# Softplus tiles in two rounded parts for the running sums, and attention scores in one VectorE pass

## The reference

```python
# sparse head: q, k, slope
logits = einsum(q, k) * 64 ** -0.5 - slope * |t - s|      # minus infinity where not selected
p = softmax(logits)
# stick-breaking head: keys s before query t only
z = einsum(q, k) * 64 ** -0.5
log_keep = log_sigmoid(-z)                                # = -softplus(z)
after = reverse cumulative sum of log_keep - log_keep
w = exp(log_sigmoid(z) + after)
```

## Time and profile before

| | us |
|---|---|
| median of 3 runs | 1257.1 (1255.69 to 1260.04) |
| the profiled execution's own time | 1256.63 |
| its span | 1254.8 |
| TensorE busy | 1225.6 |
| VectorE busy | 746.6 |
| ScalarE busy | 505.9 |
| GpSimd busy | 81.1 |
| mean granted TensorE clock | 0.995 |

### The profile page before, as it was taken

One profiled execution on the slowest core, in us unless ns is written; L12 is line 12 of the kernel. 1 busy time (PEld: TensorE's weight loads), 2 busy tenths in 40 slices (PEclk: granted clock), 3 DMA queues, 4 the chain that ended last, 5 costly groups with the idle time before them and its releaser, 6 DMA issues.

```text
span 1254.8 us, 15910 instructions
## 1 busy us (share of the span) xinstructions
PE 1225.6 (98%) x6200; PEld 993.1 (79%) x6200; DVE 746.6 (60%) x1029; ACT 505.9 (40%) x700; POOL 81.1 (6%) x122
## 2 busy tenths in 40 slices
PE   5999999999999999999999999999999999999998
PEld 4789888888888888878788875568788888888887
DVE  7998887674554444575588948755843333333332
ACT  5443426514314314334432258852551441432431
POOL 0010000000000000140000002114000000000032
PEclk9999999999999999999999999999999999999999
DMA  9558791844453454412232210003233323332211
GB/s 321 191 134 237 277 335 60 293 132 166 177 168 126 174 176 154 159 57 86 82 101 92 81 64 1 1 1 101 68 111 94 97 101 101 100 99 76 94 67 67
DMA packets 132696, 157.54 MB, mean 126 GB/s; under 512 B 19784, under 2 KB 113152, under 8 KB 132608
## 3 DMA queue, kind: packets, MB, share of 16 engines
q1 hardware_dynamic: 125328, 153.82, 36.8%
q10 hardware_dynamic: 7312, 2.96, 1.0%
HBM read 151.39 MB, written 4.19 MB: 124 GB/s over the span
## 4 chain that ended last, share of the span: by engine, by line
PE 87%; DVE 6%; DMA 3%; ACT 2%; issue 1%; ACTq 0%; POOL 0%; SPq 0%; DVEq 0%
PE psum L1800 85%; PE psum L1804 2%; DMA ada_first<-in_ada_w 1%; DVE ada_ring L1170 1%; DVE ada_acc_b L1191 1%; DMA w_raw<-in_mlp_w 1%; DMA raw_bn<-in_ssm_b_im 1%; DVE h_lo L1409 1%; ACT pT L1111 1%; DVE w_lo L1376 1%; DVE ada_acc L1191 0%; DMA y_t<-y_scratch 0%; DVE cat_f L1528 0%; DVE sumsq L1170 0%; DVE work L1390 0%
## 5 line engine op out<-in xcount | busy, mean ns | idle before, releaser
L1800 PE MATMUL psum<-h_hi,w_hi 128*128 128x512 f32 (+1 forms) x872 | 344.1, 395 | 0.6 <-DVE w_lo L1376 0.6
L1800 PE MATMUL psum<-h_lo,w_hi 128*128 128x512 f32 (+1 forms) x872 | 340.9, 391 | 0.0
L1800 PE MATMUL psum<-h_hi,w_lo 128*128 128x512 f32 (+1 forms) x872 | 340.6, 391 | 0.0
L786 ACT ACTIVATE w_hi<-w_raw 128x2048 fp32r<-128x2048 f32 x92 | 174.4, 1896 | 285.4 <-PE psum L1800 284.8
L1376 DVE TENSOR_TENSOR w_lo<-w_raw,w_hi 128x2048 fp32r<-128x2048 f32 x92 | 212.2, 2307 | 89.1 <-ACT w_hi L786 88.3
L1800 PE MATMUL psum<-a_hi,w_hi 128*128 128x512 f32 x512 | 202.5, 396 | 0.0
L1800 PE MATMUL psum<-a_hi,w_lo 128*128 128x512 f32 x512 | 202.1, 395 | 0.0
L1800 PE MATMUL psum<-a_lo,w_hi 128*128 128x512 f32 x512 | 202.1, 395 | 0.0
L1800 PEld LDWEIGHTS psum<-h_hi,w_hi 128*128 128x128 f32 (+1 forms) x872 | 164.1, 188 | 38.6 <-issue 3.6
L1800 PEld LDWEIGHTS psum<-h_hi,w_lo 128*128 128x128 f32 (+1 forms) x872 | 164.1, 188 | 35.0
L1800 PEld LDWEIGHTS psum<-h_lo,w_hi 128*128 128x128 f32 (+1 forms) x872 | 164.2, 188 | 33.3
(11 more groups left out here) (318 smaller groups left out, 1345.2 us busy)
## 6 DMA issues: line engine op xcount, KB each, us to landing
w_raw<-in_mlp_w SPq DMA_DIRECT2D x64, 1024.0 KB, 5.4
ada_l_ring<-in_ada_w SPq DMA_DIRECT2D x64, 384.0 KB, 5.9
w_raw<-in_cd_w_in SPq DMA_DIRECT2D x14, 1024.0 KB, 5.2
ada_ring<-in_ada_w SPq DMA_DIRECT2D x17, 384.0 KB, 6.0
ada_more<-in_ada_w SPq DMA_DIRECT2D x15, 384.0 KB, 4.6
ada_first<-in_ada_w SPq DMA_DIRECT2D x5, 1024.0 KB, 15.3
w_raw<-in_ab_w_in SPq DMA_DIRECT2D x4, 1024.0 KB, 7.3
w_raw<-in_ab_w_out SPq DMA_DIRECT2D x4, 1024.0 KB, 8.4
```

What stands on the lines that cost most here:

```text
L786: act.activation(w_hi[n % 2][:, :, 0:w], raw[n % 2][:, :, 0:w], ACT.Copy).then_inc(hi_ready, 1)
L1800: return nc.tensor.matmul(o, lhsT, rhs, start=start, stop=stop, **kw)
```

## The change

The softplus tile of a head is split by VectorE, behind the causal cut, in a high part in the rounded format (`sp_high`, one buffer) and a low part, the rest (`sp_low`, in the place of the tile). The running sums are then two rounded products, high and low, where one fp32 product was, with `tri` and `ones` copied once into the rounded format. TensorE waits for the split (`sp_parts`) instead of `sp_ready`.

The scores take one VectorE pass per query block: it adds the distance to the score in PSUM, multiplies with the slope, writes the result and keeps its minimum. For that the query copies carry the factor -(1/8) / slope of their head (`q_scale`, written once by eight memsets). What is written is the negated logit, so the exponential takes a scale of -1 with the minimum as its bias.

```diff
+    sp_low = [place(f"sp_low{i}", [P, W1], F32R, offset=idx_at + 4 * W1 * (2 + i)) for i in range(2)]
+    sp_high = place("sp_high", [P, W1], F32R, offset=ada_ring_at + 4 * 10 * P)
+    tri_r = place("tri_r", [P, P], F32R, offset=ada_ring_at + 4 * 20 * P)
+    ones_r = place("ones_r", [P, P], F32R, offset=ada_ring_at + 4 * 21 * P)
...
+    q_scale = small[:, 44:48]
...
@@ scalar: prob_exps, and the copies of the projection @@
-                act.activation(probs(step, i), probs(step, i), ACT.Exp, bias=small[:, i:i + 1],
+                act.activation(probs(step, i), probs(step, i), ACT.Exp, bias=small[:, i:i + 1], scale=-1.0,
                                accum_out=small[:, 8 + i:9 + i]).then_inc(p_exp, 1)
...
+                    ct = 2 * half + r
+                    if name == "qc":
+                        act.wait_ge(q_scale_ready, 1)
+                        copy_tile(t0 + r, qc[:, ct, :], scale=q_scale[:, ct:ct + 1])
+                    else:
+                        copy_tile(t0 + r, dst[:, ct, :], scale=HD ** -0.5 if name == "qd" else 1.0)
...
@@ vector, behind ada_gate(a, 16) @@
+        for t in range(4):
+            for g2 in range(2):
+                own(dve.memset(q_scale[HD * g2:HD * g2 + HD, t:t + 1], -(HD ** -0.5) / SLOPES[2 * t + g2]))
+        settle()
+        dve.sem_inc(q_scale_ready, 1)
...
@@ selected_distances @@
+            own(dve.tensor_copy(tri_r[:, :], tri[:, :]))
+            own(dve.tensor_copy(ones_r[:, :], ones[:, :]))
+            settle()
             dve.sem_inc(dsel_ready, 1)
...
+        def softplus_parts(head):
+            dve.wait_ge(sp_ready, NB * (head + 1))
+            own(dve.tensor_copy(sp_high[:, :], sp_sb[head % 2][:, :]))
+            settle()
+            dve.tensor_tensor(sp_low[head % 2][:, :], sp_sb[head % 2][:, :], sp_high[:, :].bitcast(F32), SB)\
+               .then_inc(sp_parts, 1)
...
@@ score_rows @@
-                dve.scalar_tensor_tensor(out=probs(step, i), in0=dsel[:, sel_at[i]:sel_at[i] + w],
-                                         scalar=-SLOPES[step], in1=bank[4 + n % 2][:, 0:w],
-                                         op0=M, op1=A).then_inc(s_used, 1)
-                dve.wait_ge(s_used, NB * step + n + 1)
-                dve.reduce_max(small[:, i:i + 1], probs(step, i), AX_X, negate=True)\
-                   .then_inc(max_ready, 1)
+                dve.tensor_tensor_reduce(out=probs(step, i), in0=dsel[:, sel_at[i]:sel_at[i] + w],
+                                         in1=bank[4 + n % 2][:, 0:w], scale=SLOPES[step], scalar=3.0e38,
+                                         op0=A, op1=ALU.min, accum_out=small[:, i:i + 1]).then_inc(max_ready, 1)
...
@@ vector, loop over the steps @@
             if step < H:
                 score_rows(step)
+            softplus_parts(step - 1)
             if step >= 3 and step % 2 == 1:
                 out_lo((step - 3) // 2)
...
@@ tensor: scores @@
-                pe.wait_ge(s_used, NB * step + n - 1)
+                pe.wait_ge(max_ready, NB * step + n - 1)
...
@@ stick_sums @@
-            s_ = sp_sb[pr % 2]
-            pe.wait_ge(sp_ready, NB * (pr + 1))
+            if pr == 0:
+                pe.wait_ge(dsel_ready, 1)
+            pe.wait_ge(sp_parts, pr + 1)
+            parts = (sp_high, sp_low[pr % 2])
...
-                last = mm(o[:, 0:w], tri[:, :], s_[:, z_at[j]:z_at[j] + w], True, j == NB - 1)
+                for part, s_ in enumerate(parts):
+                    last = mm(o[:, 0:w], tri_r[:, :], s_[:, z_at[j]:z_at[j] + w], part == 0, part == 1 and j == NB - 1)
                 for j2 in range(j + 1, NB):
                     w2 = (NB - j2) * P
-                    last = mm(o[:, w - w2:w], ones[:, :], s_[:, z_at[j2]:z_at[j2] + w2], False,
-                              j2 == NB - 1)
+                    for part, s_ in enumerate(parts):
+                        last = mm(o[:, w - w2:w], ones_r[:, :], s_[:, z_at[j2]:z_at[j2] + w2], False,
+                                  part == 1 and j2 == NB - 1)
```

More of the change, by code:

```diff
@@ L258, in trunk @@
     assert at[0] <= nc.sbuf_usable_end, (at[0], nc.sbuf_usable_end)
+    sp_low = [place(f"sp_low{i}", [P, W1], F32R, offset=idx_at + 4 * W1 * (2 + i)) for i in range(2)]
+    sp_high = place("sp_high", [P, W1], F32R, offset=ada_ring_at + 4 * 10 * P)
+    tri_r = place("tri_r", [P, P], F32R, offset=ada_ring_at + 4 * 20 * P)
+    ones_r = place("ones_r", [P, P], F32R, offset=ada_ring_at + 4 * 21 * P)
+    assert W1 == 10 * P and ada_ring_at + 4 * 22 * P <= ada_ring_at + 4 * (ADA_RING + 1) * ADA_Q
     p_at = [0, P, 3 * P, 6 * P]
@@ L455, in trunk @@
     sp_ready = sem("sp_ready")
+    sp_parts = sem("sp_parts")
     r_ps = sem("r_ps")
@@ L461, in trunk @@
     s_ps = sem("s_ps")
-    s_used = sem("s_used")
+    q_scale_ready = sem("q_scale_ready")
     max_ready = sem("max_ready")
@@ L875, in _ @@
         act.sem_inc(c_ready, 1)
+        qc = qk["qc"]
         def copy_tile(t, dst, src=None, **kw):
@@ L1094, in _ @@
                         continue
-                    copy_tile(t0 + r, dst[:, 2 * half + r, :], scale=HD ** -0.5 if name in ("qd", "qc") else 1.0)
+                    ct = 2 * half + r
[4 more added lines that the diff above has]
+                        copy_tile(t0 + r, dst[:, ct, :], scale=HD ** -0.5 if name == "qd" else 1.0)
                     if n == index_first and r == 0:
```

## The result

The changed kernel takes 1273.2 us (median of 4 runs, 1272.8 to 1274.7) against 1256.5 for the kernel before on the same chip (1255.7 to 1260.0); the ratio of all their runs is 1.0110, with an interval of 1.0077 to 1.0144. It is slower, by some 14 to 17 us. The forecast was 1259 with a range up to 1267: the likelier side (slower, given 0.54) came true, the size did not. The profiled execution has a span of 1271.0 us (before 1254.8) and a mean granted clock of 0.982 (before 0.995). Some single executions, of the kernel before too, take 1267 to 1275 us at a mean clock near 0.983, so times are compared as medians.

The account below looks back on a forecast made before the run. TensorE's order bounds the step, with a serial softplus chain half a microsecond behind. First step +3.4, clock +0.85, middle steps -5 x 0.02, last step -0.5, end -1.2: +2.5 on 1256.6 gives 1259 us, range 1255 to 1267.

Parts of the forecast that it names:

- the shortening: Per step, start of the sums to end of the last subtraction: 1.36 us shorter, though TensorE's sums save 1.9.
- The first step's late start: First head's sums wait for the split behind the tail of the score rows: start at 751.4, 3.4 us late.
- The end: After the last step only TensorE counts: its last sums take 3.4 us and not 4.58, -1.2.
- (a): Split's rounding copy on VectorE runs at one element a cycle: 0.66 us more in all eight steps, +5.3, 1264; chance 0.16.
- (e): Split's subtraction too runs at 0.82, so the split leaves the chain: step 11.36, 1254; chance 0.10.
- rival (c): Fused score pass on VectorE saves nothing: 1.38 x 7 = +9.7 us, 1269; chance 0.08.
- rival (b): Narrow rounded products in TensorE's sums cost the fp32 rate, 0.22: 8 x 0.45 = +3.6 us, 1263; chance 0.20.
- S = X+3.8: In each step the last subtraction ends (S) about 3.8 us after the sums start (X); before it was 5.16.
- rival (d): New TensorE idle time ahead of the sums lowers the clock in every step: 6 x 0.85 = +5 us, 1264; chance 0.08.
- From S to the next sums: Per step, end of the last subtraction through softplus, maximum, score passes, absolute value and split to the next sums: 8.22 us.
- The first, +0.85 forecast for the clock: First step's sums and what follows run partly at half speed: double the old slow spell, +0.85 us.
- The last, -0.5 forecast: Last step has no score rows: a period of 11.8 us against 12.27, -0.5.

Follow-up runs that it names:

- the filled kernel: Changed kernel plus eight unused 128-column fp32 products in TensorE's wait ahead of each step's sums; 1262.1 us, ratio 1.0042 (measured again: 1262.1, 1.0034).
- the pair: Changed kernel and the same with eight unused products in TensorE's wait, measured again side by side: 1274.7 us (9 runs) against 1262.1 (12 runs).

## Why the prediction was wrong

**Right, by the rows.** That the gain of 1.9 us in TensorE's sums would turn into a wait for the split: the wait is there in every step. That the shortening arrives as 1.36 us and not 1.9: with the clock up it was 1.38 (13.72 against 12.34). The first step's late start, 3.4 forecast, was 3.3 to 3.65. The end, -1.2, was -1.4. The copy at 0.82 and the subtraction at 1.48 were 0.83 and 1.49, so rivals (a) and (e) are out. The two tail passes took 0.63 (805.58 to 806.21), forecast 0.72; rival (c) is out. Here the Trainium skill (Vector Engine (DVE) Microarchitecture Reference, "Points that are easy to get wrong") warned that the two-source form S2S2D2_STT halves its throughput when both sources lie in SBUF and are not bf16. The fused pass has one source in PSUM and is as fast as the plain one (0.42 for 256 columns), and the maximum-and-add, with two fp32 sources in SBUF, takes the 1.49 us of the plain subtraction. The narrow rounded products: at full clock a pair of 128 columns takes 0.17 us (792.73 to 792.90), 0.06 to 0.11 each, so rival (b) is out too.

**The step that failed: S = X+3.8.** I let the sums run at full clock after 1.4 us of idle. In the filled kernel, where the clock is up, it holds: the first block takes 1.33, and S is X+3.70 (793.10 + 2.17 - 791.57). In the changed kernel the first subtraction starts at X+2.64 (798.76) and not X+1.60, and the last one ends at S = 801.24, X+5.12. This is +1.3 a step over the forecast and +1.4 over the filled kernel, and the mean steps differ by as much (13.76 - 12.34): 7.1 of the 8.65 us in the middle five intervals, and 12.6 us in the medians of the pair. It was rival (d). I gave it 0.08, on one observation, that 2 us of idle precede the drop of the earlier trace rows, which I read as if 1.4 us could then not suffice; one run shows that 1.38 can (and 1.46 need not), and the wait came out at 2.06 anyway. And I priced it at 0.85 a step, what the old first step had lost. There the slow spell began ahead of the sums and was over by 750, within their first 2 us. In the changed kernel it covers the first 3 us of the sums, and their end starts the next chain.

**A smaller term of the same sum.** From S to the next sums I had 8.22, and it was 8.54 (801.24 to 809.78), in the filled kernel 8.64 (795.27 to 803.91). The cut, which I put at 1.02 and off the path ("done since about S+5.5"), takes 1.62 beside the absolute value, ends at S+6.1 and holds the copy back; the absolute value itself was 0.98 in this step, against 0.82. The steps of 12.34 against the forecast's 12.02 show 0.32, and that is 1.9 us over the six intervals in which an absolute value runs beside the cut (in the last one the cut takes 1.03 and the term is nothing: 842.95 to 850.92, 7.97 for the 7.99 of the forecast). It also fed the first error, since it lengthens the wait, which was 2.06 and not 1.4.

**The first and the last interval.** The first, +0.85 forecast for the clock, was +1.23. The last, -0.5 forecast, was +1.46 at slow clock; with the clock up it was -0.17 (12.10 against 12.27), and there the unused products held the sums back: the split was over at 837.20 (835.71 + 1.49) and the sums started at 837.68.

**What was in no term.** The 2.57 us by which the profiled execution came late to the stage are in neither the forecast nor the change. Of the 16.2 us between the spans 13.6 belong to the stage and its end, where the forecast had 2.5.

## What to carry to other kernels

An engine that gets faster and then waits may run slower behind the wait: before pricing a new idle stretch in TensorE at its own length, look up in the trace what the granted clock does after each idle stretch of similar length, and price the products right behind it at half speed. A few unused products in the wait are a test of it, and here also a cure worth some 12 of 16 us. When two versions take the same time, compare their granted clocks before calling an edit without effect: two effects of 1.4 us a step cancelled here. Before start times of two executions are compared, they have to be set to a common point ahead of the change. Where two serial chains are half a microsecond apart, two more passes in the second one decide, and a gain in the first counts only as far as it shortens the second (here 1.38 of 1.9 us).

## What of the hardware was not expected

TensorE's clock fell to 1.2 GHz behind all eleven waits of 1.96 to 2.06 us ahead of rounded sums, in a stage where it is otherwise nearly always busy, and stayed up behind those of up to 0.97; between 1.12 and 1.54 us both were seen. With fp32 sums it also stayed up once behind 1.95 us. Four causal cuts of 128 columns on GpSimd took 1.02 us in the kernel before and with the absolute value moved away, and 1.62 to 1.71 beside it; the absolute value itself (one source, 1280 elements) took 0.98 in place of 0.82 in a step of the changed kernel.
